# Forgetting attention in one pass of scores: probabilities turned block by block instead of a second product of queries and keys

## The chip, the core and the metric

The kernel runs on one NeuronCore of a Trainium2 chip. The metric is the device time of one execution in microseconds. The core has five engines with their own instruction queues: TensorE (PE in the rows, its weight loads PEld), VectorE (DVE), ScalarE (ACT), GpSimd (POOL) and SyncE (SP). They meet only at semaphores. Matrix products land in PSUM, eight banks of 128 partitions by 512 float32; everything else lives in SBUF.

## The reference, cut to what matters

The kernel is a whole hybrid encoder block: layer norm, one input projection, two attention groups, an output projection, a routed mixture of experts. The change is in the second attention group, the forgetting attention: 8 heads of width 64, 2048 frames and 16 meta tokens that every query may see.

```python
cum = jnp.swapaxes(jnp.cumsum(log_f, axis=1), 1, 2)
for i in range(lp // Q_BLOCK):
    lo, hi = i * Q_BLOCK, (i + 1) * Q_BLOCK
    s = jnp.einsum('bqhd,bkhd->bhqk', q[:, lo:hi], k[:, :hi]).astype(jnp.float32) * (HEAD_DIM ** -0.5)
    s = s + cum[:, :, lo:hi, None] - cum[:, :, None, :hi]
    mask = (idx[None, :hi] <= idx[lo:hi, None]) & key_valid[None, :hi]
    p = jax.nn.softmax(jnp.where(mask, s, -jnp.inf), axis=-1)
    outs.append(jnp.einsum('bhqk,bkhd->bqhd', p.astype(v.dtype), v[:, :hi]))
```

The term of the query's own cumulative gate is the same for a whole row of scores and drops out of the softmax, so the kernel adds only the keys' term (`ncum`).

## The kernel before, in words

The program runs phase by phase, with a barrier between: `phase_project` (0 to about 505 us), `phase_window` (the first attention group, to about 715 us), `phase_forget` (to about 1320 us), then output projection, routing, experts and the last norm. Precise products are made of float32r matmuls on split operands: x is split into a rounded high part and the rest, and a product takes two or three matmuls.

`phase_forget` works through 32 units: head h, and in each head the groups g = 0 to 3 of 512 queries (four row tiles of 128). I write g0 to g3. For a unit it does the following.

1. `scores` (L1538 to L1544): for each row tile the scores of 128 queries against all visible keys, in chunks of up to 512 keys (`row_chunks`), two matmuls a chunk and one mask product for the last. They go to three PSUM banks `ps_r`.
2. `maxima` (L1459): VectorE adds `ncum` and takes the row maximum. The scores themselves are thrown away. `tops` splits the negated maxima, `turn_tops` (L1551) turns them into a row, and `copy_tops` (L1387) puts them under the queries' low part, so that they become two extra rows of the contraction.
3. `block_scores` (L1562 to L1570): the same scores again, now with keys on the partitions: for each block of 128 keys two matmuls over up to 512 queries, and a mask product on the diagonal, into three banks `ps_t`.
4. `exponentials` (L1395, L1396): ScalarE takes the exponential twice, once in full precision and once rounded. `probabilities_low` (L1479): VectorE subtracts the two.
5. `values` (L1582 to L1585): three matmuls a block, into `ps_o` (two banks); a column of ones in `v_hi` gives the row sums. `values` runs LAG = 4 blocks behind.
6. `copy_output`, `turn_back` (L1590) and `divide` (L1486 to L1490) bring the output back to rows; GpSimd stores it (L1352).

The order is written out by the generator `steps` (L1253): it gives every piece of work a time between 0 and 1 in its unit and sorts. Unit n's blocks are interleaved with the score chunks of unit n+1. PE, ACT and DVE walk through the same list, each doing its part, strictly in order. A unit has 4g+5 blocks; the chunks beside them are those of the next group, 9, 13, 17 and 5 for g = 0 to 3, so 44 blocks and 44 chunks a head.

A small part of the change lies in `phase_project`: a table of relative position biases is written to DRAM by a DMA (L356) in GpSimd's queue, after the third score chunk of the first 512 frames. The stores of the projected q, k and h stand behind it in the same queue. ScalarE's copies (L413) have three output slots and wait for the store of three chunks earlier.

## Time and profile before

| | |
|---|---|
| median of three runs | 2565.51 us (2565.48, 2565.51, 2572.50) |
| profiled execution | 2572.01 us, span 2570.4 us |
| mean granted clock of TensorE | 0.936 |
| PE busy over the span | 88% |
| DVE busy | 66% |
| ACT busy | 61% |
| `phase_forget` | about 719 to 1320 us |

A busy share says how long an engine held an instruction. Neighbouring instructions overlap by their pipeline ends, so the distance from one start to the next is the real price of one in a stream, and it is shorter than the duration in the row.

### The profile page before, as it was taken

How to read it: one execution, taken by the hardware profiler on the slowest of the kernel's cores; microseconds unless marked ns; L12 is line 12 of the kernel's file. 1: busy time of each engine (PE TensorE's matmuls, PEld its weight loads, DVE VectorE, ACT ScalarE, POOL GpSimd, SP SyncE). 2: the span in 40 equal slices, each digit the busy share in tenths (PEclk: the TensorE clock that was granted, in tenths of full speed). 3: DMA queues.
4: the chain of work that ended last, by engine and by line, in shares of the span. 5: the costliest groups of instructions: out<-in, count | busy, mean ns of one | idle time of the engine just before them, and what ended most of it. 6: DMA issues, size and time to landing. Idle time of an engine off the chain costs nothing. (4 is left out here: it accounts for less than half of the span.)

```text
span 2570.4 us, 35701 instructions
## 1 busy us (share of the span) xinstructions
PE 2255.2 (88%) x11310; PEld 1802.4 (70%) x11310; DVE 1700.1 (66%) x3003; ACT 1556.4 (61%) x2368; POOL 349.2 (14%) x448
## 2 busy tenths in 40 slices
PE   6989999668869999999979995499999999999970
PEld 5778888544547777777758884387888888788860
DVE  5223231166547888888743333798999999899976
ACT  4222241166638888778753332287888888788866
POOL 0111111100010000000000000122222222121211
PEclk9989999878969999999989997699999999999995
DMA  5544352242242222211033331599879778998837
GB/s 196 146 134 146 114 185 74 88 115 83 61 123 64 65 67 66 67 44 29 9 130 130 148 131 74 180 363 321 291 220 307 249 254 289 324 318 285 277 95 278
DMA packets 210017, 420.12 MB, mean 163 GB/s; under 512 B 36536, under 2 KB 86024, under 8 KB 209000
## 3 DMA queue, kind: packets, MB, share of 16 engines
q1 hardware_dynamic: 177368, 314.21, 35.8%
q0 software_dynamic: 32544, 104.58, 14.5%
q8 instruction: 57, 0.93, 0.1%
q14 instruction: 48, 0.39, 0.0%
HBM read 437.19 MB, written 86.39 MB: 204 GB/s over the span
## 5 line engine op out<-in xcount | busy, mean ns | idle before, releaser
L2420 DVE TENSOR_TENSOR moe_w_lo<-fetch_w_raw,moe_w_hi 128x1024 fp32r<-128x1024 f32 x376 | 435.6, 1219 | 12.5 <-ACT moe_w_hi L2349 12.4
L2349 ACT ACTIVATE moe_w_hi<-fetch_w_raw 128x1024 fp32r<-128x1024 f32 x376 | 369.1, 1054 | 79.4 <-DMA fetch_w_raw<-in_w_e_up_dram 39.4
L2474 PE MATMUL moe_ps_gu<-moe_w_hi,moe_xT_hi 128*128 128x512 f32 x736 | 293.3, 399 | 4.5 <-DVE moe_xT_lo L2431 4.5
L2476 PE MATMUL moe_ps_gu<-moe_w_hi,moe_xT_lo 128*128 128x512 f32 x736 | 289.4, 393 | 0.0
L2475 PE MATMUL moe_ps_gu<-moe_w_lo,moe_xT_hi 128*128 128x512 f32 x736 | 288.9, 392 | 0.0
L1395 ACT ACTIVATE fox_p<-fox_ps_t,fox_ncumT 128x512 f32<-128x512 f32 (+4 forms) x352 | 209.6, 596 | 118.2 <-PE fox_ps_t L1569 60.6
L1479 DVE TENSOR_TENSOR fox_p_lo<-fox_p,fox_p_hi 128x512 fp32r<-128x512 f32 (+4 forms) x352 | 199.6, 572 | 55.0 <-ACT fox_p_hi L1396 54.4
L1459 DVE CUSTOM_DVE_ANT_0 fox_ps_r<-fox_ps_r,fox_ncum 128x512 f32<-128x512 f32 (+4 forms) x352 | 198.2, 593 | 47.0 <-PE fox_ps_r L1539 25.9
L2426 DVE TENSOR_TENSOR moe_d_lo<-fetch_d_raw,moe_d_hi 128x1024 fp32r<-128x1024 f32 x184 | 213.1, 1220 | 10.7 <-ACT moe_d_hi L2357 8.4
L1396 ACT ACTIVATE fox_p_hi<-fox_ps_t,fox_ncumT 128x512 fp32r<-128x512 f32 (+4 forms) x352 | 207.8, 590 | 0.0
L413 ACT ACTIVATE proj_qk_out<-proj_ps_chunk 128x512 f32<-128x512 f32 x52 | 31.0, 598 | 269.8 <-PE proj_ps_chunk L623 254.6
L2357 ACT ACTIVATE moe_d_hi<-fetch_d_raw 128x1024 fp32r<-128x1024 f32 x184 | 179.5, 1058 | 0.0
L498 DVE TENSOR_TENSOR proj_w_lo<-proj_w_raw,proj_w_hi 128x2048 fp32r<-128x2048 f32 (+1 forms) x28 | 59.9, 2140 | 169.3 <-ACT proj_w_hi L405 169.3
L621 PE MATMUL proj_ps_chunk<-proj_hT_hi,proj_w_hi 128*128 128x512 f32 x416 | 165.4, 398 | 6.1 <-ACT proj_qk_out L413 5.7
L623 PE MATMUL proj_ps_chunk<-proj_hT_hi,proj_w_lo 128*128 128x512 f32 x416 | 163.7, 394 | 0.0
L622 PE MATMUL proj_ps_chunk<-proj_hT_lo,proj_w_hi 128*128 128x512 f32 x416 | 163.6, 393 | 0.0
L2474 PEld LDWEIGHTS moe_ps_gu<-moe_w_hi,moe_xT_hi 128*128 128x128 f32 x736 | 139.7, 190 | 33.7 <-DVE moe_xT_lo L2431 3.5
L2476 PEld LDWEIGHTS moe_ps_gu<-moe_w_hi,moe_xT_lo 128*128 128x128 f32 x736 | 139.5, 189 | 30.2
L2475 PEld LDWEIGHTS moe_ps_gu<-moe_w_lo,moe_xT_hi 128*128 128x128 f32 x736 | 139.6, 190 | 28.1
L2487 PE MATMUL moe_ps_y<-moe_d_hi,moe_hT_hi 128*128 128x512 f32 x368 | 148.3, 403 | 3.6 <-DVE moe_d_lo L2426 3.6
L2489 PE MATMUL moe_ps_y<-moe_d_hi,moe_hT_lo 128*128 128x512 f32 x368 | 145.2, 394 | 0.0
L2488 PE MATMUL moe_ps_y<-moe_d_lo,moe_hT_hi 128*128 128x512 f32 x368 | 144.8, 393 | 0.0
(327 smaller groups left out, 5284.2 us busy)
## 6 DMA issues: line engine op xcount, KB each, us to landing
fetch_w_raw<-in_w_e_gate_dram SPq DMA_DIRECT2D x192, 512.0 KB
fetch_w_raw<-in_w_e_up_dram SPq DMA_DIRECT2D x192, 512.0 KB
fetch_d_raw<-in_w_e_down_dram SPq DMA_DIRECT2D x92, 1024.0 KB
proj_w_raw<-in_w_in_dram SPq DMA_DIRECT2D x24, 1024.0 KB, 5.2
proj_xt<-in_x_dram SPq DMA_DIRECT2D x16, 512.0 KB
h<-proj_hrow POOLq DMA_DIRECT2D x16, 512.0 KB, 3.4
win_q_raw<-qT SPq DMA_DIRECT2D x32, 256.0 KB, 4.1
mix_o<-o SPq DMA_DIRECT2D x16, 512.0 KB, 4.4
```

What stands on the lines that cost most here:

```text
L621: nc.tensor.matmul(out, whi[:, k], hT_hi[:, k, cols], start=k == 0, stop=False)
L1395: nc.scalar.activation(p[0:keys, slot, 0:width], bank[0:keys, 0:width], ACT.Exp, bias=bias)
L1396: nc.scalar.activation(p_hi[0:keys, slot, 0:width], bank[0:keys, 0:width], ACT.Exp, bias=bias).then_inc(probs, 1)
L1459: nc.vector.tensor_tensor_reduce(out=bank, in0=bank, in1=ncum[:, h % 2, key:key + width], scale=1.0, scalar=10 * MASK, op0=ALU.add, op1=AL ...
L1479: nc.vector.tensor_tensor(p_lo[0:keys, slot, 0:width], p[0:keys, slot, 0:width], p_hi[0:keys, slot, 0:width].bitcast(F32), ALU.subtract).t ...
L2349: nc.scalar.activation(w_hi[:, k], w_raw[:, k].rearrange("p j n -> p (j n)"), ACT.Copy).then_inc(gu_high, 1)
L2357: nc.scalar.activation(d_hi[:, k], d_raw[:, k], ACT.Copy).then_inc(dn_high, 1)
L2420: nc.vector.tensor_tensor(w_lo[:, k], w_raw[:, k].rearrange("p j n -> p (j n)"), w_hi[:, k].bitcast(F32), ALU.subtract).then_inc(gu_split, 1)
L2426: nc.vector.tensor_tensor(d_lo[:, k], d_raw[:, k], d_hi[:, k].bitcast(F32), ALU.subtract).then_inc(dn_split, 1)
L2474: nc.tensor.matmul(out, xT_hi[:, slot, k], w_hi[:, k, cols], start=k == 0, stop=False)
L2475: nc.tensor.matmul(out, xT_hi[:, slot, k], w_lo[:, k, cols], start=False, stop=False)
L2476: done = nc.tensor.matmul(out, xT_lo[:, slot, k], w_hi[:, k, cols], start=False, stop=k == KT - 1)
```

## The change

- Scores are computed once, by rows. `maxima` writes score plus `ncum` into SBUF (`s`, two buffers, one for even and one for odd groups) instead of back into PSUM. The maximum is reduced per row tile (`tops`, four small reductions a unit).
- ScalarE takes one exponential in place over the row (`exponential`, pieces of up to 1040 keys, 24 a head), with the row sums as its accumulator.
- TensorE turns the probabilities by 128 x 128 blocks (`turn`, up to four transposes for a key block, four banks `ps_t`); blocks are now aligned to the queries, and the block of the 16 meta keys comes first. ScalarE copies the turned block rounded (`p_hi`), VectorE subtracts from PSUM (`p_lo`).
- `v_two` holds the values' high and low parts side by side, 128 columns, so `values` is two matmuls; the two halves of the output are added by `turn_back`, which is now four plain float32 products with `pair_sum` (two unit matrices on top of each other).
- There is one bank `ps_o` instead of two; the turned-back output takes a place in the ring of the three score banks.
- The splits of keys and queries come in four pieces instead of two; `k_one`, `q_low`, `later_r`, `cum_rows` and their work go.
- The DMA of the bias table moves from GpSimd's queue to ScalarE's, after the sixth score chunk of the second 512 frames.

```diff
-                        pool.wait_ge(table_done, 1)
-                        pool.dma_start(t["table"][:, :, 0:BIAS_TAB],
...
+                    if sb == 1 and i == 5:
+                        act.wait_ge(table_done, 1)
+                        act.dma_start(t["table"][:, :, 0:BIAS_TAB],
...
-        R_BANKS, T_BANKS = 3, 3
+        R_BANKS, T_BANKS = 3, 4
...
+        copy_at = {blocks_before[n + 1] + LAG: n for n in range(UNITS - 1)}
+        back_at = {blocks_before[n + 1] + LAG + 1: n for n in range(UNITS - 1)}
...
+            SPREAD = 0.75
...
+                    rate = SPREAD / len(ahead)
+                    events += [(rate * (i + 0.5), "scores", r) for i, r in enumerate(ahead)]
+                    for j in range(4):
+                        done = sum(len(row_chunks(4 * g + i)) for i in range(j + 1))
+                        events.append((rate * (done + 0.4), "tops", 4 * (n + 1) + j))
+                        mine = [r for r in range(pieces_before[n + 1], pieces_before[n + 2]) if pieces[r][1] == j]
+                        events += [(rate * (done + 0.8) + 0.14 * SPREAD * (i + 0.5) / len(mine), "exp", r)
+                                   for i, r in enumerate(mine)]
...
-                nc.scalar.activation(p[0:keys, slot, 0:width], bank[0:keys, 0:width], ACT.Exp, bias=bias)
-                nc.scalar.activation(p_hi[0:keys, slot, 0:width], bank[0:keys, 0:width], ACT.Exp, bias=bias
-                                     ).then_inc(probs, 1)
+                nc.scalar.activation(here, here, ACT.Exp, bias=ntop[:, n % 2, j:j + 1],
+                                     accum_out=part[g][:, j, c:c + 1]).then_inc(probs, 1)
...
+                nc.scalar.activation(p_hi[0:keys, k % P_SLOTS, skip:SBT], ps_t[k % T_BANKS][0:keys, skip:SBT], ACT.Copy
+                                     ).then_inc(p_high, 1)
...
+            def turn(k):
...
+                wait(pe, p_split, k + 1 - T_BANKS)
...
+                for j in range(skip // P, 4):
+                    if b == TILES:
+                        pe.wait_ge(probs, pieces_before[n] + sum(len(row_pieces(4 * g + i)) for i in range(j + 1)))
...
+                    done = nc.tensor.transpose(out[0:keys, j * P:(j + 1) * P], s[g % 2][:, at:at + keys], ident[:])
...
+                if b == TILES:
+                    pe.wait_ge(v_split, 2 * (h + 1))
+                    wait(pe, oT_out, n)
                 pe.wait_ge(p_split, k + 1)
-                nc.tensor.matmul(out[0:HD + 1, skip:SBT], v_hi[0:keys, u, b], high, start=b == 0, stop=False)
-                nc.tensor.matmul(out[0:HD, skip:SBT], v_lo[0:keys, u, b], high, start=False, stop=False)
-                nc.tensor.matmul(out[0:HD + 1, skip:SBT], v_hi[0:keys, u, b], low, start=False, stop=last
+                nc.tensor.matmul(out, v_two[0:keys, u, b], p_hi[0:keys, slot, skip:SBT], start=b == TILES, stop=False)
+                nc.tensor.matmul(out, v_two[0:keys, u, b], p_lo[0:keys, slot, skip:SBT], start=False, stop=b == 4 * g + 3
                                  ).then_inc(pv_done, 1)
...
-                    done = nc.tensor.transpose(ps_o[n % 2][:, j * P:j * P + HD + 1], oT[:, n % 2, j * P:(j + 1) * P],
-                                               ident[0:HD + 1, 0:HD + 1])
+                    done = nc.tensor.matmul(bank[:, j * P:j * P + HD], oT[:, n % 2, j * P:(j + 1) * P], pair_sum[:],
+                                            start=True, stop=True)
```

TensorE's queue in the middle of a g2 unit of the first head, before: two score chunks of 512 keys (L1538, L1539, into `ps_r`) and one full block (L1562 and L1565 its scores into `ps_t`, L1582 to L1584 the value products of the block four back).

```order
L1538 MATMUL fox_ps_r<-fox_k_two,fox_q_two 128x512
L1539 MATMUL fox_ps_r<-fox_k_one,fox_q_low 128x512
L1538 MATMUL fox_ps_r<-fox_k_two,fox_q_two 128x512
L1539 MATMUL fox_ps_r<-fox_k_one,fox_q_low 128x512
L1562 MATMUL fox_ps_t<-fox_q_two,fox_k_two 128x512
L1565 MATMUL fox_ps_t<-fox_q_low,fox_k_one 128x512
L1582 MATMUL fox_ps_o<-fox_p_hi,fox_v_hi 65x512
L1583 MATMUL fox_ps_o<-fox_p_hi,fox_v_lo 64x512
L1584 MATMUL fox_ps_o<-fox_p_lo,fox_v_hi 65x512
```

The same place after: the block's two score products are four transposes (one row, x4), and the three value products are two.

```order
L1474 MATMUL fox_ps_r<-fox_k_hi,fox_q_two 128x512
L1475 MATMUL fox_ps_r<-fox_k_lo,fox_q_two 128x512
L1474 MATMUL fox_ps_r<-fox_k_hi,fox_q_two 128x512
L1475 MATMUL fox_ps_r<-fox_k_lo,fox_q_two 128x512
L1490 MATMUL fox_ps_t<-ident,fox_s 128x128 x4
L1501 MATMUL fox_ps_o<-fox_p_hi,fox_v_two 128x512
L1502 MATMUL fox_ps_o<-fox_p_lo,fox_v_two 128x512
```

The score chunks are the same in both. What stands between them in a block was five matmuls of 512 columns and is now four transposes and two matmuls.

TensorE's queue at the end of that unit, where the first block of the next unit (g3) begins, after. The row with `16x128 x4` is the block of meta keys, whose transposes wait for all exponentials of the new unit.

```order
L1490 MATMUL fox_ps_t<-ident,fox_s 128x128 x2
L1501 MATMUL fox_ps_o<-fox_p_hi,fox_v_two 128x512
L1502 MATMUL fox_ps_o<-fox_p_lo,fox_v_two 128x512
L1490 MATMUL fox_ps_t<-ident,fox_s 128x128
L1501 MATMUL fox_ps_o<-fox_p_hi,fox_v_two 128x512
L1502 MATMUL fox_ps_o<-fox_p_lo,fox_v_two 128x512
L1490 MATMUL fox_ps_t<-ident,fox_s 16x128 x4
L1501 MATMUL fox_ps_o<-fox_p_hi,fox_v_two 128x512
L1502 MATMUL fox_ps_o<-fox_p_lo,fox_v_two 128x512
L1474 MATMUL fox_ps_r<-fox_k_hi,fox_q_two 128x144
L1475 MATMUL fox_ps_r<-fox_k_lo,fox_q_two 128x144
```

ScalarE's queue at the same place, after: L1343 is the exponential of a piece of a row, L1350 the rounded copy of a turned block, L1324 and L1329 splits.

```order
L1343 ACTIVATE fox_s,fox_part<-fox_s,fox_ntop 128x1040
L1350 ACTIVATE fox_p_hi<-fox_ps_t 128x512 x2
L1324 ACTIVATE fox_k_hi<-fox_k_raw 128x512
L1350 ACTIVATE fox_p_hi<-fox_ps_t 128x384
L1343 ACTIVATE fox_s,fox_part<-fox_s,fox_ntop 128x1024
L1343 ACTIVATE fox_s,fox_part<-fox_s,fox_ntop 128x1040
L1350 ACTIVATE fox_p_hi<-fox_ps_t 128x256
L1329 ACTIVATE fox_q_two<-fox_q_raw 128x512
L1350 ACTIVATE fox_p_hi<-fox_ps_t 128x128
L1350 ACTIVATE fox_p_hi<-fox_ps_t 16x512
```

Before, at the same place, L1395 and L1396 are the two exponentials of a block and L1387 the copy of the next unit's turned maxima.

```order
L1395 ACTIVATE fox_p<-fox_ps_t,fox_ncumT 128x400
L1396 ACTIVATE fox_p_hi<-fox_ps_t,fox_ncumT 128x400
L1395 ACTIVATE fox_p<-fox_ps_t,fox_ncumT 128x272
L1396 ACTIVATE fox_p_hi<-fox_ps_t,fox_ncumT 128x272
L1387 ACTIVATE fox_q_low<-fox_ps_r 2x512
L1395 ACTIVATE fox_p<-fox_ps_t,fox_ncumT 128x144
L1396 ACTIVATE fox_p_hi<-fox_ps_t,fox_ncumT 128x144
L1395 ACTIVATE fox_p<-fox_ps_t,fox_ncumT 16x16
```

What the next unit's first block waits for was one copy of the maxima, two blocks ahead of the unit's end. It is now two exponentials over more than a thousand keys each, at the same distance from the end, and behind them a split.

## Rows read from the trace of the kernel before

**Rows 1.** Windows: TensorE, weight loads, VectorE, ScalarE, GpSimd busy; granted clock; DMA share; GB/s

```profile
744.00:1316.00 572.00, 544.60 (x2986) 414.60 (x2984) 448.61 (x1236) 446.56 (x816) 34.15 (x37) 0.97 0.20 52
838.85:909.29 70.44, 66.85 (x378) 51.03 (x377) 57.01 (x158) 56.70 (x103) 4.80 (x5) 1.00 0.23 61
```

**Rows 2.** GpSimd's stores of `o`: first and last of five in one head

```profile
838.85 0.75 POOL L1352 DMA_DIRECT2D o<-fox_o  x1 [6.99 <-DVE fox_o L1489]
...
909.29 0.75 POOL L1352 DMA_DIRECT2D o<-fox_o  x1 [6.99 <-DVE fox_o L1489]
```

**Rows 3.** A wait between 722 and 1320 us: total us, times, longest

```profile
PE fox_ps_r L1551 <- DVE fox_top_two L1472: 22.6, 23, 1.3
```

**Rows 4.** TensorE in a full stream: start, duration, instruction

```profile
1201.27 0.39 PE L1538 MATMUL fox_ps_r<-fox_k_two,fox_q_two 128*128 128x512 f32 x1
1201.50 0.40 PE L1539 MATMUL fox_ps_r<-fox_k_one,fox_q_low 66*128 66x512 f32 x1
...
1202.20 0.35 PE L1582 MATMUL fox_ps_o<-fox_p_hi,fox_v_hi 128*65 128x400 f32 x1
1202.39 0.34 PE L1583 MATMUL fox_ps_o<-fox_p_hi,fox_v_lo 128*64 128x400 f32 x1
```

**Rows 5.** VectorE in a full stream, same columns

```profile
1000.16 0.68 DVE L1479 TENSOR_TENSOR fox_p_lo<-fox_p,fox_p_hi 128x512 fp32r<-128x512 f32 x1
1000.76 0.69 DVE L1459 CUSTOM_DVE_ANT_0 fox_ps_r<-fox_ps_r,fox_ncum 128x512 f32<-128x512 f32 x1
...
1001.38 0.73 DVE L1459 CUSTOM_DVE_ANT_0 fox_ps_r<-fox_ps_r,fox_ncum 128x512 f32<-128x512 f32 x1
```

**Rows 6.** VectorE subtracting out of PSUM, from the source of L2442: min/median/max ns

```profile
L2442 DVE TENSOR_TENSOR moe_hT_lo<-moe_ps_h,moe_hT_hi x46: 680/691/692, 1678.3 to 2486.1; 128x512 fp32r<-128x512 f32 x46
```

**Rows 7.** ScalarE in the last unit, where no chunks run: start, duration, instruction

```profile
1302.13 0.69 ACT L1395 ACTIVATE fox_p<-fox_ps_t,fox_ncumT 128x512 f32<-128x512 f32 x1
1302.72 0.68 ACT L1396 ACTIVATE fox_p_hi<-fox_ps_t,fox_ncumT 128x512 fp32r<-128x512 f32 x1
```

**Rows 8.** `phase_window` on TensorE: transposes, then one float32 product of 512 columns

```profile
647.20 1.04 PE L1074 MATMUL win_ps_o<-ident,win_oT 128*128 128x128 f32 x8
648.07 0.60 PE L1054 MATMUL win_ps_pT<-ident,win_s 128*80 128x128 f32 x4
...
640.66 1.04 PE L1067 MATMUL win_ps_o<-win_pT,win_v_prev 80*64 80x512 f32 x2 [0.37 <-DVE win_pT L965]
641.54 1.02 PE L1068 MATMUL win_ps_o<-win_pT,win_v_cur 128*64 128x512 f32 x2
```

**Rows 9.** `phase_window` on ScalarE: an accumulating exponential over 208 columns

```profile
640.41 0.46 ACT L872 ACTIVATE win_s<-win_s,win_ntop 128x208 f32<-128x208 f32 x1
...
640.86 0.46 ACT L872 ACTIVATE win_s<-win_s,win_ntop 128x208 f32<-128x208 f32 x1
```

**Rows 10.** Start of `phase_forget`: when the first block's scores could begin

```profile
742.97 0.77 PE L1538 MATMUL fox_ps_r<-fox_k_two,fox_q_two 128*128 128x512 f32 x1 [6.94 <-issue]
```

**Rows 11.** `phase_project`: the table's DMA, the stall behind it, and loads in that time

```profile
table<-proj_table POOLq DMA_DIRECT2D x1, 1280.0 KB, 32.2
...
proj_w_raw<-in_w_in_dram SPq DMA_DIRECT2D x2, 1024.0 KB, 29.2
...
120.09 0.60 ACT L413 ACTIVATE proj_qk_out<-proj_ps_chunk 128x512 f32<-128x512 f32 x1 [15.21 <-DMA qT<-proj_qk_out]
...
120.74 0.80 PE L621 MATMUL proj_ps_chunk<-proj_hT_hi,proj_w_hi 128*128 128x512 f32 x1 [4.71 <-ACT proj_qk_out L413]
...
141.34 0.18 PE L614 MATMUL proj_ps_chunk<-proj_mT,proj_w_hi 128*128 128x32 f32 x1
...
120.00:130.00 10.00, 7.70 (x24) 5.86 (x24) 3.36 (x2) 5.84 (x8) 0.54 (x1) 0.75 0.41 152
```

**Rows 12.** TensorE's granted clock beside its busy time in two stretches

```profile
630.00:712.00 82.00, 71.24 (x378) 41.33 (x376) 47.63 (x173) 52.65 (x169) 5.14 (x10) 1.00 0.23 67
...
965.00:970.00 5.00, 3.90 (x27) 3.00 (x26) 2.83 (x12) 2.87 (x8) 0.00 (x0) 0.80 0.00 0
```

More of the change, by code:

```diff
@@ L1269, in steps @@
                     if g in (1, 2) and head + 1 < B_HEADS:
-                        events += [((part + 0.5) / 4, "split", (head + 1, 4 * (g - 1) + part)) for part in range(4)]
+                        mine = SPLITS[4 * (g - 1):4 + 6 * (g - 1)]
+                        events += [((i + 0.5) / len(mine), "split", (head + 1, *one)) for i, one in enumerate(mine)]
                 for _, what, which in sorted(events, key=lambda event: event[0]):
                     yield what, which
-        def ring_of_row(r):
-            return r + rows[r][0]
@@ L1277, in ring_of_tops @@
-        def ring_of_tops(n):
-            return rows_before[n + 1] + n
-        tops_at = {ring_of_tops(n): n for n in range(UNITS)}
+        ring = []
+        for what, which in steps():
+            if what == "scores":
+                ring.append(("row", which))
+            elif what == "block" and which in back_at:
+                ring.append(("back", back_at[which]))
+        ring.append(("back", UNITS - 1))
+        ring_of = {use: place for place, use in enumerate(ring)}
         @block.sync
@@ L1475, in probabilities_low @@
-            def probabilities_low(k):
-                n, b, keys, skip, width, masked = blocks[k]
-                slot = k % P_SLOTS
-                dve.wait_ge(probs, k + 1)
-                nc.vector.tensor_tensor(p_lo[0:keys, slot, 0:width], p[0:keys, slot, 0:width],
-                                        p_hi[0:keys, slot, 0:width].bitcast(F32), ALU.subtract).then_inc(p_split, 1)
-            def divide(n):
-                out = ps_o[n % 2][:].rearrange("p (j d) -> p j d", d=P)
+                at = row_at[g][j] + key
@@ new lines, in maxima, with tops @@
+                nc.vector.tensor_tensor_reduce(out=s[g % 2][:, at:at + width], in0=ps_r[ring_of["row", r] % R_BANKS][:, 0:width],
+                                               in1=ncum[:, h % 2, key:key + width], scale=1.0, scalar=10 * MASK,
+                                               op0=ALU.add, op1=ALU.max, accum_out=mx[g][:, j, c:c + 1]).then_inc(biased, 1)
+            def tops(which):
+                n, j = which // 4, which % 4
+                g = units[n][1]
+                dve.wait_ge(biased, rows_before[n] + sum(len(row_chunks(4 * g + i)) for i in range(j + 1)))
+                nc.vector.tensor_reduce(ntop[:, n % 2, j:j + 1], mx[g][:, j], AX.X, ALU.max, negate=True).then_inc(maxed, 1)
@@ L1498, in _ @@
+            for what, which in steps():
                 if what == "block":
[L1499 removed]
                     if which > 0:
                         probabilities_low(which - 1)
[L1502 to L1503 removed]
+                    if which in back_at:
+                        divide(back_at[which])
                 elif what == "scores":
@@ L1517, in _, with score_bank @@
         def _(pe):
-            def row_bank_free(place):
-                last = place - R_BANKS
-                if last in tops_at:
-                    pe.wait_ge(top_ready, tops_at[last] + 1)
-                elif last >= 0:
-                    pe.wait_ge(biased, last - sum(1 for at in tops_at if at < last) + 1)
+            def score_bank(use):
+                place = ring_of[use]
+                if place >= R_BANKS:
+                    what, which = ring[place - R_BANKS]
+                    pe.wait_ge(biased if what == "row" else o_ready, which + 1)
+                return ps_r[place % R_BANKS]
             def scores(r):
@@ L1537, in scores @@
+                bank = score_bank(("row", r))
+                out, queries, keys = bank[:, 0:width], slice(i * P, (i + 1) * P), slice(key, key + width)
                 last = key + width == P * (i + 1) + META
-                nc.tensor.matmul(out[:, 0:width], q_two[:, u, queries], k_two[:, u, keys], start=True, stop=False)
-                done = nc.tensor.matmul(out[:, 0:width], q_low[0:AUG, u, queries], k_one[:, u, keys],
-                                        start=False, stop=not last)
+                nc.tensor.matmul(out, q_two[:, u, queries], k_hi[:, u, keys], start=True, stop=False)
@@ L1541, in scores @@
+                done = nc.tensor.matmul(out, q_two[:, u, queries], k_lo[:, u, keys], start=False, stop=not last)
                 if last:
-                    done = nc.tensor.matmul(out[:, width - P:width], ident_r[:], future_r[:, META:DIAG],
+                    done = nc.tensor.matmul(bank[:, width - P:width], ident_r[:], future_r[:],
                                             start=False, stop=True)
                 done.then_inc(rows_done, 1)
-            def turn_tops(n):
-                pe.wait_ge(top_split, n + 1)
-                row_bank_free(ring_of_tops(n))
-                bank = ps_r[ring_of_tops(n) % R_BANKS]
-                for j in range(4):
-                    done = nc.tensor.transpose(bank[0:2, j * P:(j + 1) * P], top_two[:, n % 2, j].bitcast(F32), ident[:])
-                done.then_inc(top_turned, 1)
```

393 lines of the change are left out of this document (146 added, 247 removed).

## Prediction

> **What bounds the kernel now.** I read the windows first, to cut the program into phases, then the waits inside `phase_forget`, then the timeline of each engine for the distance between starts. The windows show TensorE busy 544.6 of 572 us between first and last block, at a granted clock of 0.97, VectorE and ScalarE at 78% [rows 1]. One head, measured between two stores of `o` of the same group, takes 70.44 us [rows 2]. In the waits the largest that TensorE itself has in the stream is the one for VectorE's maxima before they are turned, 22.6 us or 2.8 us a head [rows 3]. So TensorE's instruction stream is the bound, and the other two have room: 57.0 and 56.7 us of 70.4 [rows 1].
>
> **Prices.** A 512-column matmul costs TensorE 0.23 us from start to start, a 400-column one 0.19 [rows 4]; that is 0.03 us and 0.4 ns a column, and I let none fall below 0.1. VectorE pays 0.62 us for a 512-column chunk of `maxima` and 0.60 for a `p_lo` [rows 5], about 0.06 us and 1.1 ns a column. A subtraction that reads PSUM lasts 691 ns [rows 6], no more than the 0.68 us that `p_lo` takes from SBUF. ScalarE pays 0.59 us for an exponential of 512 columns [rows 7]. A float32 transpose of 128 columns costs 0.11 us: eight take 0.87 us to the next instruction [rows 8].
>
> **TensorE, per head.** With these prices the old stream of a head sums to 65.5 us (8.5, 15.0, 21.5, 20.5 for g0 to g3), and 4.9 of 70.4 are stalls. Chunks of scores (18.5 us) stay.
> Removed: 28 full blocks x 2 x 0.23 = 12.9, 16 diagonal blocks of 400, 272, 144 and 16 columns 3.8, 16 mask products 1.6; the third value product, 28 x 0.23 + 1.9 = 8.3; 16 turned maxima and 16 transposes of outputs at 0.11, 3.5. Together 30.1.
> Added: 16 meta blocks and 136 real blocks make 152 transposes x 0.11 = 16.7. Blocks aligned to queries have 19,456 instead of 17,664 columns, over two products +1.4. `pair_sum`: a float32 product of 512 columns costs 0.88 us [rows 8], so 64 columns cost between 0.11 (by columns) and 0.88; these are two passes with weights of their own, nearest to two narrow matmuls, and I take 0.23, 3.7 for 16. Together 21.8.
> New sum 57 us a head (7.8, 13.3, 18.8, 16.8): 8.5 us less work. The transposes only replace the scores that they remove (4 x 0.11 against 2 x 0.23 a block); what is gained is the third value product and the masks.
>
> **VectorE, per head.** The old stream sums to 54.0 (7.1, 15.1, 20.0, 11.8). Added: 1,792 columns of `p_lo` 1.9, sixteen small reductions for four groups of three 0.7, the row totals 0.7. New 57.3 (7.9, 15.9, 20.8, 12.7). Writing the chunk's result to SBUF instead of PSUM is not shown for this width; from 0 to +0.06 us a chunk, 0 to 2.6 us a head, and I take 0 because the subtraction of rows 6 doesn't care either.
> **ScalarE**: two exponentials over 17,664 columns go (42 us), one over SBUF and one copy of 19,456 columns come. An accumulating exponential of 208 columns starts 0.45 us before the next [rows 9], so 24 pieces cost about 0.27 each beside 0.83 ns a column: 21, and the copies 19 to 23. ScalarE stays below 50 us a head, but in g2 it is at about 17 of 20.8.
>
> **So the bound changes hands.** Unit by unit the larger of TensorE and VectorE is 7.9, 15.9, 20.8, 16.8: 61.4 us a head instead of 65.5. VectorE binds in g1 and g2.
>
> **What is late next** is the handover. The first transposes of a unit wait for all exponentials of that unit; behind them in TensorE's queue stand the value products and the next chunks, for which VectorE waits. The chain from VectorE's last chunk is: reduction 0.17, two exponentials of 1024 and 1040 columns 2.3 (one of 1040, 1.15, in g1), transposes 0.45, copy 0.5. VectorE has only 2.0 us of other work behind the last reduction of g2 and 1.1 of g1. I get: g1 and g2 together 39.3 instead of 36.7 to the first transpose of g3; g0 9.4 instead of 7.9; and one bank `ps_o`, for which the first value product waits while ScalarE copies 512 columns (0.6 us, beside four transposes at 0.45), 0.4 in the TensorE-bound unit. That is 4.5. Of the old stalls, the 2.8 behind the turned maxima go and 2.1 I keep. 61.4 + 4.5 + 2.1 = 68.0 us a head against 70.4: 2.4 x 8 = 19 us. In g1 and g2 TensorE will stand still for about 3 us at the end of the unit, since it runs ahead of VectorE.
>
> **Start of the phase.** The first block began at 742.97, after keys and queries 1536 columns wide had been split [rows 10]. The splits are the same amount in pieces, but the first unit no longer waits for turned gates or maxima, and pieces of 512 let the second unit start sooner: -5 us, between -2 and -7.
>
> **The table's DMA.** It takes 32.2 us; key weights loaded beside it took 29.2 us. A store of `qT` behind it made ScalarE wait 15.21 us and TensorE 4.71, and then TensorE ran at 0.75 of its clock [rows 11]. ScalarE's copy before the wait began at 120.09 - 15.21 - 0.60 = 104.28, when a chunk had just ended; a chunk is 24 matmuls or 5.45 us, so TensorE went on until 115.2 and stood until 120.74. The next two chunks, the second with sixteen small meta products (1.8 us), would have ended at 115.2 + 5.45 + 7.25 = 127.9, and TensorE comes to the products behind them at 141.34 [rows 11]: 13.4 us lost. In ScalarE's own queue no store stands behind the table, but loads still share the DMA engines for 32 us. At the new place the next weights have about 18 us until ScalarE rounds them, and two more chunks before TensorE needs them. So the loss is between 0 and all 13.4, and I take 4.4: -9 us.
> The Trainium skill (SBUF — State Buffer, on the port swizzle) says that DMA bandwidth depends on how many of the 16 ports the partitions reach; the table leaves from 8 partitions, two ports, 54 GB/s, so the estimate by that page is 24 us whichever queue issues it. The trace agrees in kind (1280 KB in 32.2 us, 41 GB/s), and nothing in the sum above rests on it.
>
> **Sum.** 2572.0 (the profiled execution) - 19 - 5 - 9 = 2539, rounded 2540. The median of the runs, 2565.5, lies 6.5 us below the profiled execution, as two of three runs did; I don't subtract that and leave it in the range. What a measurement can tell from no change is 0.3%, 7.7 us: 2557.8 to 2573.2 counts as the same.
>
> **Rivals.**
> A. *The handover is hidden.* TensorE and VectorE slide against each other (three score banks, four turned banks), and a head costs its bound, 61.4, plus 2 = 63.5: 6.9 x 8 = 55, start -5, table -9 to -13: 2500. For it: g0 and g3 leave VectorE slack to catch up. Against: all three queues are strict, and g2 loads all three above 80%. 0.17.
> B. *VectorE pays more.* +0.06 a chunk and more stall at the handover, 70 a head; the table's stall comes back at its new place: 2572 - 3 - 5 - 2 = 2562. No change. For it: 44 blocks and 44 chunks now all pass through banks that VectorE must empty last. 0.15.
> C. *The clock falls* (slower). TensorE idles about 3 us at two handovers a head. Before, after 4.71 us of waiting the clock was 0.75 over 10 us [rows 11], and at 965 to 970, busy 3.90 of 5 us, it was 0.80 [rows 12]. If each handover costs 5 us at 1.2 GHz, 2.5 us of TensorE's work are lost each time: 5 a head, 73 in all, +21 - 5 - 4 = 2584. It decides from 4.1 us a head on, where the 33 us of gain are gone. Against it: in `phase_window` TensorE is busy 71 of 82 us with pauses in each tile and kept 1.00 [rows 12]. 0.17.
> D. *Transposes keep the clock down.* In the g3 unit transposes are nearly half of TensorE's time. At 1.2 GHz that unit would take 34 instead of 17 us, +17 x 8 = 136: about 2680. Against it: `phase_window` has 24 transposes a tile, a quarter of TensorE's time, at 1.00 [rows 8, 12]. 0.04.
> The Trainium skill (TensorE: Matmul & The Clock Gate, Part 4) states the mechanism of D: the full clock "doesn't engage for transpose-mode". The trace of `phase_window` does not agree, where transposes are mixed with products.
> The forecast (2515 to 2557) gets 0.47.
>
> **Chances and range.** Faster: the forecast and A, less the part of the forecast near its edge: 0.62. Same: B: 0.15. Slower: C, D and a remainder: 0.23. The range goes from 63 us a head with all of the table's gain (2500) to 73 (2582).
>
> **What would show it.** A head between stores of `o` of the same group: 68 (61 to 65 for A, 73 for C). VectorE busy near 61 us a head by records, TensorE's waits moved from L1551 to the transposes L1490 behind ScalarE's L1343, about 3 us each, in g2 to g3 above all. Four transposes at 0.44. In the projection, no wait of L413 for a store at 104 us, and a shorter one, if any, after 215. I am wrong if TensorE's transposes cost clearly more than 0.11 in a mixed stream, if the `pair_sum` products cost over 0.4, or if the granted clock in the phase is below 0.95.

## The result, and the profile after

The changed kernel takes 2584.58 us (median of 4 runs, 2580.25 to 2586.39), the kernel before in the same comparison 2566.87: a ratio of 1.0063, interval 1.0047 to 1.0079. It is slower by 0.63%, where I had forecast 2540. The profiled execution took 2586.11 us (span 2584.0, granted clock 0.929 against 0.936).

First the windows of the changed kernel, a stretch of the phase (its last 15 us are left out) and one head (between two stores of `o` of the same group). They answer to [rows 1, 2]; the columns are the same.

```profile
744.00:1320.00 576.00, 494.31 (x2850) 402.44 (x2848) 434.98 (x1285) 386.21 (x801) 22.60 (x30) 0.92 0.18 46
911.82:987.46 75.64, 64.61 (x380) 52.55 (x378) 57.61 (x171) 50.91 (x106) 3.01 (x4) 0.93 0.22 57
```

The stretches of [rows 1] and of this view don't hold the same work, so I compare from the first to the last store of `o`, which do. Before, TensorE is busy 521.0 of 549.8 us there, at a granted clock of 0.99; after, 496.2 of 578.2 us, at 0.93. It has less to do, and the phase is longer. The head shown takes 75.6 us instead of 70.4. VectorE is busy 57.6 us in it by records, before 57.0; my sum of 57.3 was by starts, and I had expected near 61 by records, so VectorE has about 3 us less to do than I forecast. ScalarE is at 50.9 by records, for "below 50" by starts.

The waits of TensorE between 700 and 1400 us show where it stands (us in total, times, longest). L1501 is the first product of values with probabilities of a unit, L1490 the transposes, L1474 the scores; they answer to [rows 3].

```profile
PE fox_ps_o L1501 <- issue: 53.6, 31, 3.1
PE fox_ps_t L1490 <- ACT fox_s L1343: 24.3, 19, 1.9
PE fox_ps_r L1474 <- DVE fox_q_two L1385: 13.8, 1, 13.8
PE fox_ps_r L1474 <- issue: 7.4, 1, 7.4
PE fox_ps_r L1474 <- DVE fox_mx L1404: 4.4, 15, 0.7
PE fox_ps_t L1490 <- DVE fox_p_lo L1417: 1.8, 7, 0.3
```

The largest, 53.6 us, has "issue" as its releaser, which means that the profile shows nothing that the engine waited for. The timeline names it. Here is ScalarE at a change from g3 to g0, and TensorE's first product behind it (start, us, what; in brackets the idle time before it).

```profile
1041.68 0.36 ACT L1350 ACTIVATE fox_p_hi<-fox_ps_t 128x256 fp32r<-128x256 f32 x1
1042.59 1.16 ACT L1343 ACTIVATE fox_s<-fox_s,fox_ntop 128x1040 f32<-128x1040 f32 x1 [0.55 <-DVE fox_ntop L1412]
1043.66 0.19 ACT L1343 ACTIVATION_READ_ACCUMULATOR fox_s<-fox_s,fox_ntop 128x1 f32 x1
1043.75 0.58 ACT L1356 ACTIVATE fox_oT<-fox_ps_o 128x512 f32<-128x512 f32 x1
```
```profile
1040.57 0.28 PE L1502 MATMUL fox_ps_o<-fox_p_lo,fox_v_two 128*128 128x128 f32 x1
1044.43 0.76 PE L1501 MATMUL fox_ps_o<-fox_p_hi,fox_v_two 16*128 16x512 f32 x1 [3.11 <-issue]
```

TensorE starts the last product of the old unit at 1040.57. With its end the single bank `ps_o` is ready to be copied, but in ScalarE's queue an exponential of 1040 columns stands ahead of the copy, and that one waits 0.55 us for its maximum. The copy starts at 1043.75, and the first product of the new unit 0.68 us later. The other unit changes have waits of 1.3 to 2.0 us into g1, 2.0 into g2 and 0.2 into g3 (less in the last head): 7.3 us of 75.64 in the head shown.

What such a wait does to the clock is in the windows of 5 us around it (the last three columns are granted clock, DMA share and GB/s).

```profile
1040.00:1045.00 5.00, 1.89 (x13) 1.58 (x11) 2.86 (x11) 3.60 (x8) 0.00 (x0) 0.86 0.00 0
1045.00:1050.00 5.00, 5.00 (x19) 3.64 (x18) 1.15 (x5) 1.11 (x2) 0.00 (x0) 0.50 0.00 0
1050.00:1055.00 5.00, 5.00 (x23) 4.49 (x23) 3.63 (x11) 1.52 (x4) 0.75 (x1) 0.61 0.11 26
1055.00:1060.00 5.00, 3.35 (x23) 2.73 (x22) 4.96 (x16) 4.94 (x11) 0.00 (x0) 1.00 0.00 0
1080.00:1085.00 5.00, 5.00 (x24) 4.32 (x24) 3.53 (x12) 3.17 (x6) 0.13 (x1) 0.66 0.00 0
```

Behind the 3.11 us wait TensorE runs at 0.50 (the lower of the two levels, 1.2 GHz) for a whole window and at 0.61 in the next, with 19 and 23 matmuls, where the windows from 955 to 965 at full clock have 33 and 36; behind the 2.0 us wait that ended at 1079.13 it is 0.66 for one window.

### The profile page after: what moved, and what is told of

It reads as the page before. It is cut to its first block and busy times, and to the rows that moved or that the text cites. A ratio compares the mean times of both kernels' runs of the same rounds, so it can differ in the third digit from the quotient of the medians.

```text
span 2584.0 us, 35970 instructions
## 1 busy us (share of the span) xinstructions
PE 2215.3 (86%) x11293; PEld 1802.5 (70%) x11293; DVE 1704.9 (66%) x3112; ACT 1510.4 (58%) x2389; POOL 331.3 (13%) x435
## 3 DMA queue, kind: packets, MB, share of 16 engines
q0 software_dynamic: 32016, 103.26, 13.9%
q10 hardware_dynamic: 1032, 1.31, 0.4%
## 5 line engine op out<-in xcount | busy, mean ns | idle before, releaser
L2330 DVE TENSOR_TENSOR moe_w_lo<-fetch_w_raw,moe_w_hi 128x1024 fp32r<-128x1024 f32 x376 | 435.5, 1218 | 12.8 <-ACT moe_w_hi L2259 12.5
L1350 ACT ACTIVATE fox_p_hi<-fox_ps_t 128x512 fp32r<-128x512 f32 (+4 forms) x352 | 185.2, 532 | 146.8 <-PE fox_ps_t L1490 146.0
L1404 DVE CUSTOM_DVE_ANT_0 fox_s<-fox_ps_r,fox_ncum 128x512 f32<-128x512 f32 (+4 forms) x352 | 193.8, 568 | 64.3 <-PE fox_ps_r L1475 57.0
L1490 PE MATMUL fox_ps_t<-ident,fox_s 128*128 128x128 f32 (+1 forms) x1216 | 204.4, 283 | 27.0 <-ACT fox_s L1343 24.3
L1417 DVE TENSOR_TENSOR fox_p_lo<-fox_ps_t,fox_p_hi 128x512 fp32r<-128x512 f32 (+4 forms) x352 | 210.6, 610 | 11.5 <-ACT fox_p_hi L1350 10.6
L1501 PE MATMUL fox_ps_o<-fox_p_hi,fox_v_two 128*128 128x512 f32 (+4 forms) x352 | 164.6, 468 | 53.6 <-issue 53.6
L1343 ACT ACTIVATE fox_s<-fox_s,fox_ntop 128x144 f32<-128x144 f32 (+5 forms) x192 | 173.3, 903 | 55.5 <-DVE fox_ntop L1412 55.2
L1490 PEld LDWEIGHTS fox_ps_t<-ident,fox_s 128*128 128x128 f32 (+1 forms) x1216 | 144.9, 139 | 73.1 <-ACT fox_s L1343 30.0
L1474 PE MATMUL fox_ps_r<-fox_k_hi,fox_q_two 128*128 128x512 f32 (+4 forms) x352 | 142.9, 406 | 25.7 <-DVE fox_q_two L1385 13.8
```

The costliest lines, as they stand in the source:

```text
L1343: nc.scalar.activation(here, here, ACT.Exp, bias=ntop[:, n % 2, j:j + 1], accum_out=part[g][:, j, c:c + 1]).then_inc(probs, 1)
L1350: nc.scalar.activation(p_hi[0:keys, k % P_SLOTS, skip:SBT], ps_t[k % T_BANKS][0:keys, skip:SBT], ACT.Copy).then_inc(p_high, 1)
L1404: nc.vector.tensor_tensor_reduce(out=s[g % 2][:, at:at + width], in0=ps_r[ring_of["row", r] % R_BANKS][:, 0:width], in1=ncum[:, h % 2, key ...
L1417: nc.vector.tensor_tensor(p_lo[0:keys, k % P_SLOTS, skip:SBT], ps_t[k % T_BANKS][0:keys, skip:SBT], p_hi[0:keys, k % P_SLOTS, skip:SBT].bi ...
L1490: done = nc.tensor.transpose(out[0:keys, j * P:(j + 1) * P], s[g % 2][:, at:at + keys], ident[:])
L2330: nc.vector.tensor_tensor(w_lo[:, k], w_raw[:, k].rearrange("p j n -> p (j n)"), w_hi[:, k].bitcast(F32), ALU.subtract).then_inc(gu_split, 1)
```

## The experiments

All are compared with the kernel before on the same chip; "ratio" is to it, with its interval. Its medians in these sessions were 2565.5 (e1 to e4), 2565.9 (e5 to e8), 2567.3 (e9 to e12) and 2566.4 us (e13 to e16). Differences between two experiments are between their medians; taken from the ratios they come out up to 3 us different, for instance 30 us instead of 32 between e3 and e5.

**The table alone (e1)**: the kernel before, and only the table's DMA moved as in the change.

> The kernel before with nothing changed but the table's DMA, issued by ScalarE after chunk 5 of the second block instead of by GpSimd in the first. Theory: the move is worth in itself what the trace of the changed kernel shows at the start of phase_forget (709.8 us instead of 719.3), so 2566.9 - 9.5 = 2557, ratio 0.9963. Rival: part of that came from the new phase_forget or shifts back later (a load that is late at the new place); then 2560 to 2567, ratio 0.997 to 1.000.

Measured 2562.8 us, ratio 0.9990 (0.9977 to 1.0003). The rival holds: hardly any gain. ScalarE's waits for DMAs between 60 and 300 us in the changed kernel show why:

```profile
ACT proj_junk L376 <- DMA proj_xt<-in_x_dram: 11.8, 1, 11.8
ACT proj_qk_out L410 <- DMA qT<-proj_qk_out: 5.8, 1, 5.8
```

The second, for a store of `qT`, ends at 252.18, and TensorE has no wait behind it. The first, for a load of `x`, ends at 264.62. ScalarE's copy of the chunk stands behind it in its queue, and TensorE waits for that copy:

```profile
264.62 1.06 ACT L376 ACTIVATE proj_junk<-proj_xt 128x1024 bf16<-128x1024 f32 x1 [11.84 <-DMA proj_xt<-in_x_dram]
```
```profile
267.90 0.80 PE L622 MATMUL proj_ps_chunk<-proj_hT_hi,proj_w_hi 128*128 128x512 f32 x1 [7.68 <-ACT proj_qk_out L410]
```

The stall of [rows 11] is gone at 120 us and a stall is back at 260, 7.68 us long, with another transfer behind it: a late load of `x` in SyncE's queue instead of a late store of `qT`. The profile of e1 has the same two waits, 11.3 and 6.5 us, and the kernel before has none for `x`. While the table is on its way other transfers take longer. A store of `qT` of 128 KB takes 8.9 us instead of 3.1, and loads of weights a median of 18.6 instead of 5.2. The rows are of the stores of `qT` issued between 230 and 290 us, before and after:

```profile
qT<-proj_qk_out POOLq DMA_DIRECT2D x8, 128.0 KB, 3.1
```
```profile
qT<-proj_qk_out POOLq DMA_DIRECT2D x6, 128.0 KB, 8.9
```

**Two output banks (e2)**, at the price of the fourth turned bank, **and its control (e3)**, three turned banks and still one output bank.

```diff
-R_BANKS, T_BANKS = 3, 4
+R_BANKS, T_BANKS = 3, 3
-ps_o = m.ps("ps_o", [P, 512])
+ps_o = [m.ps(f"ps_o{i}", [P, 512]) for i in range(2)]      # e2 only; unit n uses ps_o[n % 2]
-wait(pe, oT_out, n)
+wait(pe, oT_out, n - 1)                                    # e2 only
```

> The changed kernel with two banks for the value products (a unit writes the bank that the unit before it does not use) and three banks instead of four for turned probabilities. Theory (the single output bank, and the clock that falls behind its waits): the waits at L1501 (2.0 to 3.1 us at three of four unit changes, 53.6 us in all) go, the granted clock of the phase rises from 0.92 to 0.96 or more, a head takes 66 to 69 us instead of 75.5: 2584.6 - 8 x 7.5 = 2525, between 2505 and 2540. Rival 1 (the order is bound by VectorE and ScalarE anyway, the waits only move to the transposes and score banks): a head keeps 73 to 75.5, 2565 to 2584. Rival 2 (three turned banks are too few): slower than 2584, and the kernel with three turned banks and one output bank shows the same loss.

> The changed kernel with three banks for turned probabilities instead of four and still one output bank: the control of the kernel with two output banks. Theory: a fourth turned bank matters little beside the waits for the output bank, within 0.3% of the changed kernel, 2577 to 2592. Rival: the fourth bank was what kept the waits at the transposes (24.3 us) small; then above 2600.

Measured 2536.6 us for e2, ratio 0.9884 (0.9865 to 0.9903), and 2603.3 for e3, ratio 1.0139 (1.0120 to 1.0158). The second output bank is worth 66.7 us against its control. Windows of e3 and of e2, and the waits of e2:

```profile
744.00:1320.00 576.00, 492.79 (x2755) 396.24 (x2753) 423.49 (x1250) 374.26 (x779) 21.82 (x29) 0.91 0.18 46
```
```profile
744.00:1290.00 546.00, 486.81 (x2950) 386.58 (x2950) 444.47 (x1309) 392.66 (x820) 23.36 (x31) 0.99 0.20 51
```
```profile
PE fox_ps_t L1490 <- ACT fox_s L1343: 21.3, 26, 1.9
PE fox_ps_t L1490 <- DVE fox_p_lo L1417: 19.8, 28, 1.3
PE fox_ps_r L1474 <- DVE fox_mx L1404: 13.3, 34, 0.7
PE fox_ps_r L1474 <- DVE fox_o L1430: 5.2, 7, 0.8
```

The wait at L1501 is gone. The waits of the stream add up to 86 us in e3 (52.7 of them at L1501) and to 60 in e2: 27 us less of 66.7. The other 40 I put down to the clock, which rose from 0.91 to 0.99 over 550 us; that is a remainder and not a measurement, and e5 below measures it. Of e3 I had expected no change; it lost 19 us, the range of its rival. The rival's mechanism, longer waits at the transposes, is hardly there: L1490 waits 28.7 us in all (14.8 for the exponentials, 13.9 for `p_lo`) instead of 26.1, and all waits of the stream are 86 instead of 84. Between first and last store of `o` e3 has the same 2884 matmuls in its records as the changed kernel but is busy with them 13.5 us longer (509.7 for 496.2, clock 0.92 for 0.93), so most of the loss is in slower work and not in waits; what slows it beyond the clock stays open.

**The copy first (e4)**: one bank, four turned banks, and only the copy's place in ScalarE's order changed.

```diff
-if which in copy_at:
-    copy_output(copy_at[which])
 probabilities_high(which)
+if which + 1 in copy_at:
+    copy_output(copy_at[which + 1])
```

> The changed kernel with ScalarE's copy of the outputs moved ahead of the one or two exponentials that stand between it and the copy of the probabilities before it; all else, one output bank too, as it was. Theory: the wait at L1501 is the copy's place behind exponentials of 640 to 1040 columns (0.9 us each), so 1.8 us less at the change to g1 and 0.9 to 1.1 less at those to g2 and g3: 3.8 us a head directly, and the clock falls less; 2584.6 - 8 x 5 = 2545, between 2530 and 2555. Rival: the delayed exponentials make the next unit's maxima or transposes as much later, no change (2578 to 2590).

Measured 2539.2 us, ratio 0.9900 (0.9881 to 0.9918), 45 us less than the changed kernel. Its wait at L1501, and ScalarE's same place, where the copy now starts right behind `p_hi` and the exponential behind the copy:

```profile
PE fox_ps_o L1501 <- issue: 18.9, 28, 1.3
```
```profile
1084.36 0.36 ACT L1350 ACTIVATE fox_p_hi<-fox_ps_t 128x256 fp32r<-128x256 f32 x1
1084.62 0.58 ACT L1356 ACTIVATE fox_oT<-fox_ps_o 128x512 f32<-128x512 f32 x1
1085.27 1.16 ACT L1343 ACTIVATE fox_s<-fox_s,fox_ntop 128x1040 f32<-128x1040 f32 x1
```

53.6 us became 18.9, the longest 1.3; the clock of the phase is 0.97. The delayed exponentials cost little (26.9 us at L1490 instead of 24.3).

**Unread products in the wait (e5, e14) and behind it (e13)** tell what the clock costs by itself. On e3, which has a bank free, six (e5, e13) or three (e14) 512-column products are added that nobody reads; e13 has the same ones, but behind the wait.

```diff
+if n > 0 and g < 3:
+    for _ in range(6):
+        nc.tensor.matmul(ps_d[:], ident_r[:], ident_r[:].unsqueeze(1).to_broadcast([P, 4, P]), start=True, stop=True)
 wait(pe, oT_out, n)
```

> The kernel with three turned banks and one output bank (2603, clock 0.91 in the phase), with six 512-column products ahead of TensorE's wait for the copy of the outputs, into the bank that is free there, at the starts of g1, g2 and of g0 from the second head on. Nobody reads what they write; they take about 1.4 us of waits of 2.0 to 3.1 us. Theory: the clock falls because TensorE stands still there, and what it costs is 10 to 20 us of the 45 that the early copy gave: clock 0.95 or more, 2585 to 2593. Rival: the clock's fall costs nothing, since TensorE waits for the others anyway: 2600 to 2606 with a higher clock. Second rival: the products delay the chain: above 2606.

> The kernel with three turned banks and one output bank (2603) and the same six unread 512-column products as in the kernel that came to 2571, but behind TensorE's wait for the copy instead of ahead of it. Same work, but it fills no wait. Theory (the gain of 32 us came from TensorE not standing still, so that the clock stayed up): no such gain, and the products' own time on top, 23 x 1.4 us or more: 2603 + 32 = 2635, between 2620 and 2660, clock 0.93 or less. Rival (the products help in some other way, by their place among the weights or by shifting VectorE): below 2595.

> Three instead of six of the unread products ahead of the wait, 0.7 us of waits of 2.0 to 3.1. Theory: the waits into g1 and g2 keep 1.3 us, which kept the clock at 1.00 elsewhere (1.83 us at 965.55 in the kernel with the early copy), the one into g0 keeps 2.4 and lets it fall: two thirds of the effect of six, 2575 to 2588. Rival: any filled part helps in proportion: half, 2584 to 2590. Second rival: the fall hangs on the wait into g0 alone: 2595 to 2603.

Measured: e5 2570.9 us, ratio 1.0024 (1.0015 to 1.0032); e13 2628.1, 1.0237 (1.0223 to 1.0251); e14 2584.0, 1.0065 (1.0051 to 1.0079). So 138 useless products made the kernel 32 us faster where they fill a wait, and 25 us slower behind it: 57 us for nothing but their place. Half as many gave 19 of the 32; 2584.0 fits both my theory of e14 (2575 to 2588) and its rival (2584 to 2590), so e14 doesn't tell whether the gain is in proportion. Windows of e5, around the same unit change, and the whole phase of e5 and of e13:

```profile
1040.00:1045.00 5.00, 4.42 (x24) 3.13 (x22) 4.20 (x13) 4.02 (x10) 0.00 (x0) 1.00 0.00 0
1045.00:1050.00 5.00, 4.42 (x29) 3.35 (x28) 3.74 (x12) 3.44 (x9) 0.75 (x1) 1.00 0.11 26
1050.00:1055.00 5.00, 4.22 (x25) 3.09 (x24) 3.63 (x9) 3.69 (x8) 0.00 (x0) 1.00 0.34 79
744.00:1310.00 566.00, 509.83 (x3027) 406.97 (x3026) 438.51 (x1285) 389.15 (x805) 23.37 (x31) 0.98 0.19 47
```
```profile
744.00:1365.00 621.00, 535.91 (x2993) 423.63 (x2992) 435.25 (x1286) 387.46 (x802) 22.57 (x30) 0.93 0.17 43
```

The dip to 0.50 is gone and the phase has 0.98. e5 did better than I expected (10 to 20 us); its remaining waits at the bank (21 us) and the products (138 x 0.23 = 32) add up to the 53 us that e3 waits there, so the copy comes no sooner, and the 32 us gained (30 by the ratios) are what most of the clock's fall costs, from 0.91 back to 0.98.

**Does anything stand behind the first cause? (e7, e8, e10, e11)** On the early copy: the next unit's rows spread over 0.65 (e7) or 0.85 (e10) of a unit instead of 0.75, and the early copy with two output banks (e8). On the changed kernel: two output banks taken from the score ring, `R_BANKS, T_BANKS = 2, 4` (e11).

> The kernel with the early copy (2539), and the next unit's scores, maxima and exponentials spread over the first 0.65 of a unit instead of 0.75. Theory of the handover: the first transposes wait for the last exponential (1.3 to 1.8 us at the changes to g2 and g3, 3.2 us a head), since VectorE and ScalarE have too little behind the last row; sooner rows take these waits away: 2515 to 2530. Rival: VectorE and ScalarE are then later with the probabilities of the present unit, and the waits move to the score and turned banks: 2535 to 2555.

> The kernel with the early copy (2539), with the next unit's rows spread over 0.85 of a unit instead of 0.75 (0.65 gave 2553). Theory: TensorE and VectorE slide less against each other, but the last exponentials come later, so the waits of the first transposes grow from 3.2 us a head: 2540 to 2560, 0.75 is near the best. Rival: rows spread still more evenly keep helping: below 2533.

> Two output banks, three turned banks, and the early copy together. Theory: both edits remove the same wait (alone 2536.6 and 2539.2), so together no more than one of them: 2530 to 2545. Rival: the copy's place behind the exponentials costs something else too (the turned-back outputs in the ring come sooner), another 8 to 15 us less: 2521 to 2529.

> The changed kernel with two output banks, taken from the score ring (two score banks, four turned banks) instead of the turned banks. Theory: with two banks of outputs the wait and the fall of the clock go, but VectorE's 0.62 us a chunk then stands between two chunks on TensorE: waits at L1474 for fox_mx grow from 13 to over 30 us; 2540 to 2565. Rival: four turned banks are worth more than the third score bank (a fourth turned bank was worth 19 us with one output bank): below 2530.

Measured: e7 2553.6 us, ratio 0.9946 (0.9934 to 0.9959); e10 2552.4, 0.9942 (0.9922 to 0.9961); e8 2538.8, 0.9901 (0.9886 to 0.9915); e11 2533.8, 0.9872 (0.9852 to 0.9892). Rows sooner or later both lose 13 to 14 us (11 to 12 by the ratios). The largest wait of TensorE in e7 and in e10:

```profile
PE fox_ps_t L1490 <- DVE fox_p_lo L1417: 26.9, 16, 3.3
```
```profile
PE fox_ps_t L1490 <- ACT fox_s L1343: 55.3, 26, 3.4
```

Sooner rows put VectorE's `p_lo` late (3.3 us in e4), later rows the exponentials (26.9 in e4). In e7 the wait for the exponentials did fall to 12.3, but my theory of a gain failed: the waits moved, as its rival had it. It held in e10. e8 shows that the early copy and the second bank remove the same thing. e11 pays for its bank with 25.5 us at the score ring (`fox_mx`, 13.3 in e2), less than the over 30 that I had expected, and saves e2's 19.8 behind `p_lo`. Its time lies below my range (2540 to 2565) and above its rival's (below 2530).

**The table, settled (e6, e9, e15)**: the kernel before with the table in eight pieces of 16 destination rows, one behind each of the chunks 0 to 7 of the second block (e6); the changed kernel with the table at its old place (e9); the kernel before once more for a second profile (e15).

> The kernel before with nothing changed but the table's DMA: eight pieces (16 of 128 destination rows each, 164 KB) from ScalarE, one after each of the chunks 0 to 7 of the second block. Theory: the whole table in one DMA of 1280 KB holds up a store of qT by 5 to 8 us wherever it is put, so the move alone gave 2.7 us of the 13 lost at the old place; a piece lasts about 4 us of every 5.4 and holds nothing up: 2553 to 2558, ratio 0.995 to 0.997. Rival: the gain is limited by something else in the projection, then as the move alone, 2560 to 2564.

> The changed kernel with the table's DMA back on GpSimd's queue in the first block. Theory: the move is worth what it was worth in the kernel before, 2.7 us (up to 6), since the same stall of 7 us comes back at the new place: 2585 to 2591. Rival (my prediction): the move is worth 9 us: 2592 to 2596.

> The kernel before, unchanged, for a second profile. The two profiles at hand have phase_forget begin 9.5 us apart, while moving the table measured 2.7 us in one kernel and 1 to 3 in the other. Theory: the profiled execution of before was a late one (2572 against a median of 2566), so this one has phase_forget begin 2 to 6 us sooner than 719.3. Rival: it begins at 719 again, and the 9.5 us are given back behind that place.

Measured: e6 2553.1 us, ratio 0.9948 (0.9935 to 0.9960), and ScalarE waits for no DMA between 60 and 300 us in it. The gain is as I expected, but my theory named the wrong transfer at the new place: what cost TensorE time there was the load of `x`, not a store of `qT`. The others: e9 2585.9, 1.0076 (1.0058 to 1.0094), against 1.0063 for the changed kernel; e15 2564.8, 0.9990 (0.9980 to 1.0000). The same instruction of ScalarE, the first of `phase_forget`, in e15 and in the changed kernel:

```profile
715.65 0.32 ACT L1405 ACTIVATE fox_future_r<-fox_future 128x144 fp32r<-128x144 f32 x1 [8.96 <-POOL fox_later L1332]
```
```profile
710.55 0.31 ACT L1359 ACTIVATE fox_future_r<-fox_future 128x128 fp32r<-128x128 f32 x1 [8.70 <-POOL fox_future L1306]
```

In the first profile of before it started at 720.40: two executions of one kernel differ by 4.75 us here, half of the 9.5 that the first pair of profiles shows. By the runs the move is worth 2.7 us in e1 (interval -0.8 to 5.9) and 1.3 in e9 (3.3 by the ratios, whose intervals overlap); cut in pieces it is worth 12.8.

**A faster version (e12, e16)**: the early copy with the table in pieces (e12), and both with two output banks out of the score ring (e16).

> The changed kernel with the early copy and the table's DMA in eight pieces. Theory: both gains add, 2539.2 - (12.8 - 2.7) = 2529, between 2524 and 2533, ratio to the kernel before 0.984 to 0.988: faster than both kernels. Rival: the projection's gain is lost again at the next boundary: 2535 to 2541.

> Two output banks out of the score ring (two score banks, four turned banks), the early copy, and the table's DMA in eight pieces. Theory: the banks kernel came to 2533.8 with the table in one piece, the pieces are worth 9 to 10, the early copy nothing beside two banks: 2524, between 2519 and 2528, the fastest so far. Rival: it ends where the one with the early copy and pieces did, 2528 to 2533.

Measured: e12 2530.3 us, ratio 0.9853 (0.9833 to 0.9873); e16 2523.8, 0.9834 (0.9821 to 0.9847). Both beat both kernels. The phase of e16:

```profile
735.00:1270.00 535.00, 484.31 (x2918) 379.30 (x2919) 441.62 (x1302) 392.77 (x814) 23.37 (x31) 0.99 0.21 52
```

## Why the prediction was wrong

**The step that failed** is the one on `ps_o`: "one bank `ps_o`, for which the first value product waits while ScalarE copies 512 columns (0.6 us, beside four transposes at 0.45), 0.4 in the TensorE-bound unit". I priced the copy and not its place in ScalarE's queue. It stands there behind exponentials of 640 to 1040 columns, which themselves can wait for VectorE (0.55 us at 1042.59). The wait is 6.7 us a head (53.6 / 8), at three unit changes of four. The second part of the step is the clock behind idle time, which my sum put at nothing, although it had TensorE standing still for about 3 us in g1 and in g2: I had it in rival C alone. With 0.92 in the phase my own sign of being wrong, a clock below 0.95, came true. By e5 the clock costs about 32 us, in the kernel with three turned banks. Together wait and clock are what e4 takes back by moving the copy alone: between first and last store of `o` the changed kernel takes 578.2 us (757.21 to 1335.36) and e4 535.1 (751.64 to 1286.77), 43 us or 5.4 a head.

**The rest of the heads came near in sum, in part by luck.** Between those stores the kernel before takes 552.8 us (e15) or 549.8 (its first profile), so e4 is 15 to 18 us faster; I had forecast 19 with a single-bank wait of 0.4. But I had forecast eight heads of 68.0 us for 70.4. In e4 the first seven take a mean of 70.3 us (69.3 to 71.9), for 71.3 and 71.7 in the two profiles of before, 1.0 to 1.5 less each. The other 7 us come from the stretch behind the last head's first store, 43.4 us instead of 50.7, which my sum didn't treat by itself. e4 also still waits 18.9 us at L1501, 2.4 a head where I had 0.4.

The prices of TensorE hold in sum in the changed kernel. These rows are one block and the start of the next, from TensorE's timeline:

```profile
955.24 0.60 PE L1490 MATMUL fox_ps_t<-ident,fox_s 128*128 128x128 f32 x4
955.60 0.48 PE L1501 MATMUL fox_ps_o<-fox_p_hi,fox_v_two 128*128 128x512 f32 x1
955.92 0.40 PE L1502 MATMUL fox_ps_o<-fox_p_lo,fox_v_two 128*128 128x512 f32 x1
956.15 0.27 PE L1490 MATMUL fox_ps_t<-ident,fox_s 128*128 128x128 f32 x1
```

A block is 0.91 us from transposes to transposes, against 4 x 0.11 + 2 x 0.23 = 0.90. The parts differ: the transposes take 0.36, the first product behind them 0.32 and the second 0.23. The four `pair_sum` products of a unit, eight passes, take 0.81 us (from 947.83 to the next instruction at 948.64), 0.20 each for the 0.23 that I chose between 0.11 and 0.88. A slip in my sum was small: by my own prices the diagonal blocks cost 4.2 and not 3.8, and the third value product of them 2.1 and not 1.9. VectorE's chunk, written to SBUF, has a mean of 684 ns by the groups of the page for the 711 that it had with PSUM: the +0.06 that I had left open is not there. Whether VectorE binds g1 and g2, as I had it, no run shows, since none changed its work; it is busy 57.2 us by records in e4's head of 69.4 (961.31 to 1030.69).

**The handover** to the exponentials was too dear: TensorE waits 1.3 to 1.4 us at two changes of the head shown (24.3 us in all at L1490) where I had about 3 each. I had looked for TensorE's idle time at the transposes; it was at the first product.

**The start** was forecast at -5 us: from ScalarE's first instruction to the first store of `o` the kernel before takes 48.1, the changed one 46.7, e4 42.8 (from 708.83). The start was right once the same wait was gone.

**The table** was forecast at -9 and the profiles showed -9.5, which was no confirmation: the runs say 1 to 3 us. That the loss at the old place is 13 us was right (e6: 12.8 with pieces); that only 4.4 come back at the new place was wrong, about 10 do. I had looked at the stores and at the next weights there, and not at the load of `x`, for which ScalarE waits 11.84 us. Part of rival B ("the table's stall comes back at its new place") is what happened.

**Rival C** gave the time, 2584, and its mechanism was there, with other numbers: I had two idles of 3 us a head at the handovers and 2.5 us of clock each, 73 us a head. There are three waits at the output bank, of 2.0, 2.0 and 3.1 us, and a head takes 75.6 us (74.5 to 79.5 in the seven). The clock's own part is 32 us by e5. I gave C 0.17 and its place was wrong, since my own sum held nothing that would stop TensorE at the bank. That the number fits is in part luck: seven heads cost 5.0 us each more than in the first profile of before (mean 76.3 for 71.3), where C had 2.6, and the stretch behind the last head's first store costs 6.3 less. Rival D is out: e2 has as many transposes as the changed kernel and a clock of 0.99 over 546 us.

The Trainium skill (TensorE: Matmul & The Clock Gate, Part 4), which I had cited for D, is not borne out by that row of e2, where transposes are mixed with products. What lowered the clock here were TensorE's waits, by e5 and e13.

What stays open: why the fourth turned bank is worth 19 us with one output bank, beyond what the clock explains, and what makes executions of the same kernel begin `phase_forget` 5 us apart.

## What to carry to other kernels

Where a change leaves one bank between two units, price the wait by the queue of the engine that empties it: everything that stands ahead of the copy in its order, with that engine's own waits, not the copy's duration. Price an idle time of TensorE inside a busy stretch by more than its own length: here waits of 53 us in all came with about 32 us more for the clock behind them. Where one large DMA moves to another place, go through every transfer that is on its way at that time, loads too. A difference between two profiles is worth as much as two executions of one kernel agree at that place; take a second profile of before, or run the edit alone.

## What the hardware did that I had not expected

Unread matmuls can pay: 138 of them, about 32 us of work placed in waits of mostly 2.0 to 3.1 us, shortened the kernel by 32 us, while the same ones outside the waits lengthened it by 25. After a wait of 3.1 us the granted clock was 0.50 and 0.61 in the two 5 us windows behind it, after one of 2.0 us 0.66 in one window. Shorter ones go either way: in e4 a wait of 1.83 us that ended at 965.55 left it at 1.00, one of 1.31 us that ended at 1085.31 was followed by a window of 0.66. One DMA of 1280 KB from 8 partitions stopped TensorE wherever it was issued. From GpSimd's queue it did so by way of a late store, 4.7 and 2.3 us in the first profile of before and 3.3 and 2.7 in e15; from ScalarE's queue by way of a late load, 7.7 us. The same bytes in eight pieces of 160 KB left no wait for a DMA, and the kernel was 12.8 us faster.
